# Stick attention with stationary values: fp32r value products over two query tiles, weights turned in two rounded parts

## The reference, cut to what matters

```python
for blk in range(S // SB_BLOCK):            # 8 blocks of 128 queries
    z = einsum('bthd,bshd->bhts', q[:, q0:kend], k[:, :kend]) * d ** -0.5
    strict = s_idx < t_idx
    log_beta = log_sigmoid(z)
    log_one_minus = where(strict, log_sigmoid(-z), 0.0)
    suffix = cumsum(log_one_minus, axis=3, reverse=True) - log_one_minus
    w = where(strict, exp(log_beta + suffix), 0.0)
    outs.append(einsum('bhts,bshd->bthd', w, v[:, :kend]))
```

## Time and profile before

| | |
|---|---|
| median of 2 runs | 2490.82 us (2488.91 to 2492.73) |
| profiled execution | 2491.72 us, its span 2489.9 us |
| mean granted TensorE clock over the span | 0.949 |
| busy over the span: PE, PEld | 2234.8 us (90%), 1854.2 us (74%) |
| busy over the span: DVE, ACT, POOL | 1336.9 us (54%), 1095.4 us (44%), 562.9 us (23%) |
| stick stage | first scores at 1620.67 us, last output copy at 1796.06 us |

### The profile page before, as it was taken

One profiled execution on the slowest core, in us unless ns is written; L12 is line 12 of the kernel. 1 busy time (PEld: TensorE's weight loads), 2 busy tenths in 40 slices (PEclk: granted clock), 3 DMA queues, 4 the chain that ended last, 5 costly groups with the idle time before them and its releaser, 6 DMA issues. The chain is left out here.

```text
span 2489.9 us, 34790 instructions
## 1 busy us (share of the span) xinstructions
PE 2234.8 (90%) x12528; PEld 1854.2 (74%) x12528; DVE 1336.9 (54%) x2212; ACT 1095.4 (44%) x2028; POOL 562.9 (23%) x598
## 2 busy tenths in 40 slices
PE   8997898899899899999589999688889999967778
PEld 6786787799887766676478887678777878856667
DVE  3332666688654666666541210777675434428843
ACT  3231545688632355554441210266543333328641
POOL 1002200723011122332210000466421000017821
PEclk9999899999999899999799999889989999988889
DMA  4686965633253599998553211453152543141152
GB/s 159 188 253 172 248 187 153 189 78 67 67 189 117 224 362 372 354 347 320 188 192 111 96 66 51 129 136 75 53 192 79 161 145 113 72 141 46 44 195 93
DMA packets 216904, 399.78 MB, mean 161 GB/s; under 512 B 90560, under 2 KB 111424, under 8 KB 204080
## 3 DMA queue, kind: packets, MB, share of 16 engines
q1 hardware_dynamic: 177184, 315.04, 39.9%
q10 hardware_dynamic: 28384, 61.62, 6.5%
q0 software_dynamic: 11184, 21.13, 2.4%
HBM read 300.68 MB, written 114.85 MB: 167 GB/s over the span
## 5 line engine op out<-in xcount | busy, mean ns | idle before, releaser
L78 PE MATMUL pe_acc<-pe_w,hT 128*128 128x512 f32 x960 | 229.5, 400 | 12.8 <-DVE hT L762 11.5
L78 PEld LDWEIGHTS pe_acc<-pe_w,hT 128*128 128x128 f32 x960 | 183.4, 192 | 55.9 <-DVE hT L762 14.1
L78 PE MATMUL ex_gu<-hT,ex_xT 128*128 128x512 f32 x792 | 196.4, 404 | 1.7 <-DVE hT L2666 1.7
L2666 DVE TENSOR_TENSOR hT<-ex_raw,hT 128x2048 fp32r<-128x2048 f32 x66 | 150.9, 2288 | 80.5 <-ACT hT L2637 80.5
L78 PE MATMUL pg_acc<-hT,pg_w 128*128 128x512 f32 x768 | 178.5, 393 | 0.9 <-DVE pg_w L286 0.9
L78 PEld LDWEIGHTS ex_gu<-hT,ex_xT 128*128 128x128 f32 x792 | 148.8, 191 | 35.9 <-DVE hT L2666 1.9
L78 PEld LDWEIGHTS pg_acc<-hT,pg_w 128*128 128x128 f32 x768 | 143.9, 188 | 34.1 <-issue 2.9
L2637 ACT ACTIVATE hT<-ex_raw 128x2048 fp32r<-128x2048 f32 x66 | 126.2, 1914 | 31.9 <-PEq L47 20.6
L325 DVE COPY pe_o<-pe_acc 128x512 f32<-128x512 f32 x28 | 19.3, 690 | 207.1 <-PE pe_acc L78 207.0
L2595 PE MATMUL ex_dn<-ex_wd,ex_hT 128*128 128x512 f32 x264 | 118.8, 593 | 0.8 <-ACT ex_hT L2631 0.8
L78 PE MATMUL pa_acc<-hT,pa_w 128*128 128x512 f32 (+1 forms) x432 | 100.6, 392 | 3.4 <-DVE pa_o L319 1.9
(11 more groups left out here) (545 smaller groups left out, 5355.2 us busy)
## 6 DMA issues: line engine op xcount, KB each, us to landing
ex_raw<-in_w_gate SPq DMA_DIRECT2D x33, 1024.0 KB, 7.3
ex_raw<-in_w_up SPq DMA_DIRECT2D x33, 1024.0 KB, 10.7
ex_wd<-in_w_down SPq DMA_DIRECT2D x33, 1024.0 KB, 13.7
ex_raw<-in_even_w_in SPq DMA_DIRECT2D x6, 2048.0 KB, 8.8
pg_raw<-in_odd_w_in SPq DMA_DIRECT2D x5, 2048.0 KB, 9.3
scr_q<-pa_o SPq DMA_DIRECT2D x32, 256.0 KB, 3.9
scr_k<-pa_o SPq DMA_DIRECT2D x32, 256.0 KB, 3.8
hT<-scr_k SPq DMA_DIRECT2D x16, 512.0 KB, 7.0
```

What stands on the lines that cost most here:

```text
L78: mm = pe.matmul(out, a(p, k), b(q, k), start=(k == 0 and i == 0), stop=(k == n - 1 and i == 2))
L2666: dve.tensor_tensor(split(s, LO)[:, :, g, :], raw[:, s % NW, g, :].rearrange("p (k n) -> p k n", k=8), split(s, HI)[:, :, g, :].bitcast(F3 ...
```

## The change

The value product is turned round. The values become the stationary operand: `vs` holds for each key block 128 columns, 64 of the values rounded to fp32r (ACT, 3149) and 64 of the remainder (POOL, 3239). The turned weights stream, as a rounded part that ACT writes (3170, 3173) and a remainder that DVE subtracts (3204, 3208). The product runs once for two query blocks, over 256 columns, in step T for the pair that ends with unit T-4, on odd steps (3123). On the last key block only the second query block streams, over 128 columns. The result has the two parts of the values in its partitions 0 to 63 and 64 to 127 and the queries in its columns. ACT drains it to `oT` (3163) one step later. TensorE turns it back and adds the two parts with a stacked identity (3134) in step T for the pair that ends with T-6. DVE copies both blocks to the output buffer in the step after (3224). The last step of a unit is thus three steps later than before.

```diff
--- before.py
+++ after.py
@@ -2988,7 +2988,10 @@
         be = st.sb("sb_be", [P, 4, S])
         pr = st.sb("sb_pr", [P, 2, S + 1])
         w = st.sb("sb_w", [P, 4, S])
-        wT = st.sb("sb_wT", [P, 2, S])
+        vs = st.sb("sb_vs", [P, 2, NT, 2 * DV], F32R)
+        wT = st.sb("sb_wT", [P, 2, 2, NT, 2 * P], F32R)
+        oT = st.sb("sb_oT", [P, 2, 2 * P])
+        stack = st.sb("sb_stack", [P, DV])
         ones = st.sb("sb_ones", [P, S])
         masks = st.sb("sb_masks", [P, 2, P])
         far = st.sb("sb_far", [P, P], F32R)
@@ -2996,20 +2999,30 @@
         o = st.sb("sb_ob", [P, 2, NT, DV])
         sps = [st.ps(f"sb_s{s}", [P, S]) for s in range(2)]
         tps = st.ps("sb_t", [P, S])
-        ops = [st.ps(f"sb_op{s}", [P, BANK]) for s in range(2)]
+        pvs = st.ps("sb_pv", [P, 2 * P])
+        ops = st.ps("sb_op", [P, 2, P])
...
+        def part_of(q, m, kk):
+
+            return wT[:, m // 2 % 2, q, kk, m % 2 * P:m % 2 * P + P]
+
+        def turned(kk):
+
+            return tps[:, kk.start * P:kk.stop * P].rearrange("p (k n) -> p k n", n=P)
 
         with nc.Block() as block:
             @block.sync
@@ -3046,7 +3059,7 @@
                         sp.sem_inc(passed, 1)
                         load_raw(h + 2, u)
                         store(h, u)
-                        sp.wait_ge(pv_done, h * T8 + T8)
+                        sp.wait_ge(vl_ok, h * T8 + T8)
                         sp.sem_inc(passed, 1)
                         load_v(h + 2, u)
                 store(heads - 2, 0)
@@ -3084,8 +3097,8 @@
                         m = (l - 3) % TURN
                         a, b = halves(m % T8)
                         reached(pe, w_ok, T - 2)
-                        reached(pe, wT_a, T - 3)
-                        reached(pe, wT_b, T - 3)
+                        reached(pe, wTl_a, T - 3)
+                        reached(pe, wTl_b, T - 3)
                         for k in range(b):
                             mm = pe.transpose(tps[:, k * P:(k + 1) * P], w[:, m % 4, k * P:(k + 1) * P], ident[:, :])
                             if k == a - 1 and b > a:
@@ -3096,19 +3109,31 @@
                             mm.then_inc(turned_a, 1)
                             pe.wait_ge(turned_a, T - 2)
                             pe.sem_inc(turned_b, 1)
-                    if active(T, 4, total):
-                        m = (l - 4) % TURN
-                        u, i = m // T8, m % T8
-                        if i == 0:
-                            pe.wait_ge(v_in[u], T - 4 - 8 * u + 16)
-                        reached(pe, o_done, T - 5)
-                        reached(pe, wT_a, T - 3)
-                        reached(pe, wT_b, T - 3)
+                    m = (l - 4) % TURN
+                    if active(T, 4, total) and m % 2 == 1:
+                        u, i, x = m // T8, m % T8, m // 2 % 2
+                        if i == 1:
+                            pe.wait_ge(vl_ok, T + 3)
+                        reached(pe, oT_ok, T - 5)
+                        reached(pe, wTl_a, T - 3)
+                        reached(pe, wTl_b, T - 3)
                         for k in range(i + 1):
-                            mm = pe.matmul(ops[m % 2][:, 0:DV], wT[:, m % 2, k * P:(k + 1) * P], v[:, u, k, :],
-                                           start=(k == 0), stop=(k == i))
-                        mm.then_inc(pv_done, 1)
-                tiles(pe, total, 8, 4, body)
+                            both = slice(P if k == i else 0, 2 * P)
+                            for q in (HI, LO):
+                                mm = pe.matmul(pvs[:, both], vs[:, u, k, :], wT[:, x, q, k, both], start=(k == 0 and q == HI),
+                                               stop=(k == i and q == LO), skip_group_check=True)
+                        mm.then_inc(pv_done, 2)
+                    m = (l - 6) % TURN
+                    if active(T, 6, total) and m % 2 == 1:
+                        x = m // 2 % 2
+                        if isinstance(T, int) and T == 7:
+                            pe.wait_ge(stack_ok, 3)
+                        reached(pe, oT_ok, T - 5)
+                        reached(pe, o_done, T - 7)
+                        for a in range(2):
+                            mm = pe.matmul(ops[:, a, 0:DV], oT[:, x, a * P:a * P + P], stack[:, :], start=True, stop=True)
+                        mm.then_inc(back, 2)
+                tiles(pe, total, 8, 6, body)
                 keep_clock(pe, sps[0], ident, 12)
 
             @block.scalar
@@ -3118,6 +3143,10 @@
                     act.wait_ge(raw_in[u], n_in)
                     act.activation(qs[:, u, :], qraw[:, u, :], ACT.Copy).then_inc(hi_ok, 4)
                     act.activation(kh[:, u, :], kraw[:, u, :], ACT.Copy).then_inc(hi_ok, 4)
+
+                def split_v(u):
+
+                    act.activation(vs[:, u, :, 0:DV], v[:, u, :, :], ACT.Copy).then_inc(vh_ok, T8)
 
                 def body(l, T):
                     if active(T, 0, total):
@@ -3127,21 +3156,36 @@
                         act.activation(be[:, l % 4, 0:n], sps[l % 2][:, 0:n], ACT.Sigmoid, scale=0.125).then_inc(be_ok, 1)
                         act.wait_ge(be_ok, T + 1)
                         act.activation(sps[l % 2][:, 0:n], sps[l % 2][:, 0:n], ACT.Sigmoid, scale=-0.125).then_inc(om_ok, 1)
+                    m = (l - 5) % TURN
+                    if active(T, 5, total) and m % 2 == 1:
+                        reached(act, pv_done, T - 4)
+                        reached(act, back, T - 8)
+                        act.activation(oT[:, m // 2 % 2, :], pvs[:, :], ACT.Copy).then_inc(oT_ok, 2)
                     if active(T, 3, total):
                         m = (l - 3) % TURN
                         a, b = halves(m % T8)
+                        if m % 2 == 0:
+                            reached(act, pv_done, T - 5)
+                        reached(act, turned_a, T - 2)
+                        act.activation(part_of(HI, m, slice(0, a)), turned(slice(0, a)), ACT.Copy).then_inc(wTh_a, 1)
                         reached(act, turned_b, T - 2)
                         if b > a:
-                            reached(act, pv_done, T - 4)
-                            act.activation(wT[:, m % 2, a * P:b * P], tps[:, a * P:b * P], ACT.Copy).then_inc(wT_b, 1)
+                            act.activation(part_of(HI, m, slice(a, b)), turned(slice(a, b)), ACT.Copy).then_inc(wTh_b, 1)
                         else:
-                            act.sem_inc(wT_b, 1)
+                            act.sem_inc(wTh_b, 1)
                     if active(T, 0, total):
                         if l % T8 == 3 and active(T + 5, 0, total):
 
                             u = 1 - l // T8
                             split_hi(u, (T + 5 - 8 * u) * 4 + 64)
-                tiles(act, total, 8, 4, body)
+                        if isinstance(T, int) and T < 2:
+                            act.wait_ge(v_in[T], 16)
+                            split_v(T)
+                        if l % T8 == 6 and active(T + 2, 0, total) and not (isinstance(T, int) and T < T8):
+                            u = 1 - l // T8
+                            act.wait_ge(v_in[u], T + 2 - 8 * u + 16)
+                            split_v(u)
+                tiles(act, total, 8, 5, body)
 
             @block.vector
             def _(dve):
@@ -3155,28 +3199,52 @@
                 def body(l, T):
                     if active(T, 3, total):
                         m = (l - 3) % TURN
-                        a, _ = halves(m % T8)
-                        reached(dve, turned_a, T - 2)
-                        reached(dve, pv_done, T - 4)
-                        dve.tensor_copy(wT[:, m % 2, 0:a * P], tps[:, 0:a * P]).then_inc(wT_a, 1)
+                        a, b = halves(m % T8)
+                        reached(dve, wTh_a, T - 2)
+                        dve.tensor_tensor(part_of(LO, m, slice(0, a)), turned(slice(0, a)), part_of(HI, m, slice(0, a)).bitcast(F32),
+                                          ALU.subtract).then_inc(wTl_a, 1)
+                        reached(dve, wTh_b, T - 2)
+                        if b > a:
+                            dve.tensor_tensor(part_of(LO, m, slice(a, b)), turned(slice(a, b)), part_of(HI, m, slice(a, b)).bitcast(F32),
+                                              ALU.subtract).then_inc(wTl_b, 1)
+                        else:
+                            dve.sem_inc(wTl_b, 1)
                     if active(T, 0, total):
                         n = widths[l % T8]
                         dve.wait_ge(om_ok, T + 1)
                         reached(dve, w_ok, T - 1)
                         dve.tensor_tensor_scan(pr[:, l % 2, S - n:S][:, ::-1], sps[l % 2][:, 0:n][:, ::-1], ones[:, 0:n], 1.0,
                                                ALU.mult, ALU.mult).then_inc(pr_ok, 1)
-                    if active(T, 4, total):
-                        m = (l - 4) % TURN
-                        u, i = m // T8, m % T8
```

(36 more changed lines are left out.)

## The result

| | before | after |
|---|---|---|
| median of 2 runs | 2490.82 us | 2598.10 us (2595.98 to 2600.21) |
| profiled execution, its span | 2491.72, 2489.9 us | 2595.98, 2593.9 us |
| mean granted TensorE clock | 0.949 | 0.935 |
| stick stage, first scores to last output copy | 175.6 us | 278.6 us |

A forecast was written before the change was run, and what follows sets the result against it. The loop scan, scores, sigmoids, scan was taken to end last, becoming one longer chain. Chain 33.1, first head 2.4, load 42.0, start 3.9, end 2.0, clock 15.9 + 2 on 2491.72 gave 2593.0, less 0.9: 2592 us, range 2562 to 2618.

The forecast's parts named there:

- load wait: Before the sigmoids of step 7, ACT waits for the DMA of the values: 7.0 us, six times, 42.0.
- steps 0, 1: Subtractions of tile 5, handover, seven turns, 12 products, turns back: 3.61 us a head, 2.65 more at half clock.
- steps 6, 7: Scores, sigmoids, drain, copies, rounded values, subtractions and scan in one chain: 9.94 us a head, besides the values' load.
- first head: Half the chain's cost, 2.4 us, as steps 0 to 2 lack earlier tiles, plus 3.9 for the second values.
- The chain: Side-by-side work becomes one chain round a head: 25.8 against 21.1 us, 4.7 a head, 33.1 over seven heads.
- rival 1: TensorE's relief decides, with copies and loads hidden: 2486 us, not slower; chance 0.03.
- The clock: After each values' wait, half clock in steps 0 and 1 adds 2.65 us, six times 15.9; short waits add 2.
- 2 for the short waits: The clock allowance for short waits, beside the 15.9 after the values' waits: 2 us in all.
- rival 4: The clock stays low well beyond step 1: 2605 to 2626 us; chance 0.16.
- The start: In step 1 ACT waits for the second values, ahead of the sigmoids of step 2: 3.9 us.
- The end: After the last scan, the last tiles pass through turn, copy, subtraction, products, drain, turns back and copy: 2.0 us more.
- The signs: Blocks 0 of heads 3 to 8 about 33 to 36 us apart, head 8 about 26; six ACT waits near 7 us.

The follow-up runs named there:

- e1: The changed kernel with the values of head h+2 loaded ahead of the store of head h on SP; 2551.07 us, ratio 1.0249.
- e7: e1 without DVE's subtractions, still 40 products a head, the high parts multiplied twice; 2517.62 us, ratio 1.0095.
- e6: e1 with subtractions kept but low parts of the turned weights not multiplied, 20 products a head, not 40; 2545.75 us, ratio 1.0213.
- e2: The changed kernel with 24 throwaway TensorE matmuls in the load waits of heads 3 to 8, and also in head 2; 2602.80 us, ratio 1.0440.
- e9: The changed kernel with 24 throwaway TensorE matmuls only in the load waits of heads 3, 5 and 7; 2596.56 us, ratio 1.0432.
- e3: e1 with DVE's scan of each step made ahead of that step's two subtractions; 2571.84 us, ratio 1.0331.

## Why the prediction was right

The four legs of a head, from the starts and ends of the rows above. "Full clock" are the shortest values of e1 in heads 3 to 7, where no load wait stands in them; they come from different heads, and no head of e1 had all four (its shortest took 27.59 us). Before, steps 2, 3 and 4, 5 are 5.83 and 4.03 us, the other four steps 11.2.

| leg | forecast | full clock (e1) | after, head 5 |
|---|---|---|---|
| steps 0, 1 (last scan's end to scores of step 2) | 3.61 + 2.65 clock | 3.89 | 5.51 |
| steps 2, 3 | 6.75 | 6.88 | 6.88 |
| steps 4, 5 | 5.54 | 5.64 | 5.64 |
| steps 6, 7 | 9.94 + 7.0 load | 9.88 | 17.34 |
| head | 25.8 + 9.65 | 26.3 | 35.4 |

| term | forecast | measured |
|---|---|---|
| chain, seven heads | 33.1 | 36.6 = 7 x 26.29 - 147.4 |
| values' load, six times | 42.0 | 43.4 = 42.8 of idle + 6 x 0.09 |
| clock | 15.9 + 2 | 16.6, what is left of 244.0 - 147.4 |
| start of the stage | 0 | 2.3 |
| first head | 3.9 + 2.4 | 2.2 |
| end | 2.0 | 4.2 = (1901.58 - 1889.85) - 7.5 |
| behind the stage | 0 | -1.3 |
| sum | 101.3 | 104.0 |

- **The chain** was right to 0.5 us a head, and each leg to 0.3. e7 confirms its largest part, the subtractions. The rule in the Trainium skill ("Perfetto Trace Analysis", "Identifying the Most-Contended Engine") to relieve the fullest engine first would have given rival 1's 2486. Here the fullest engine was relieved, at the price of work for the others, and the time rose by 107 us; e6 shows what TensorE's work is worth on this chain, 5 to 8 us for half of the products.
- **The load wait** was right in place, number and size. e1 removes it.
- **The clock** was right in sum by luck and wrong in cause, which is the step of the prediction that failed: the turns, products and turns back of steps 0 and 1 "come next on the chain; at half clock they add 2.65, six times 15.9". They did not double: in e1 the turns took 1.6 times as long, the products 1.8 times, and the turns back, by which time the clock was rising again, no longer (1706 to 1708 stood at 0.50, 1709.5 to 1710 at 1.00). From scan to the scores of step 2 the changed kernel took 4.86 to 5.60 us in heads 3 to 8, 7.9 above six times 3.89, half of the 15.9. But the clock falls in every head at least once, in short idle times of the new chain, with or without the load wait: in e1 the remainder that I put down to it is 11 us over heads 2 to 8 (their 195.1 us against 7 x 26.29). So "2 for the short waits" was far too little, and the two errors cancelled. The load wait's own share would be the rest, some 5 or 6; no run isolates it, and e2, less its 4 us in head 2, got nothing back. The Trainium skill's warning of short idle times between groups of matmuls ("TensorE: Matmul & The Clock Gate", "A second HAM failure mode: psum-queue depth-cycling"), which I had given to rival 4, is what e9's windows agree with.
- **The start** was over-estimated. The wait for the second values was 2.32 us, not 3.9, and head 1 grew by 2.2 instead of 6.3: it is slow before, too, with its clock at 0.50 from 1626 to 1634. That the stage began 2.3 us later says nothing: in the profiled executions of e3 and e2, with the same program ahead of the stage, it began at 1616.8 and 1630.7.
- **The end** had its turn (1.73) and product (2.21) at a granted clock of 0.55 to 0.59; I had counted them at full. By the rows of e1 that is some 1.3 of the 2.2 us missed; the rest was not taken apart.
- **The signs** that I named: blocks 0 of heads 3 to 8 stand 35.2 to 38.2 us apart (33 to 36 forecast), and by their last scans heads 3 to 7 are 35.1 to 38.1. The largest is head 3, outside the forecast: its clock fell a second time and was 0.50 from 1694 to 1704. Head 8 is 27.9 (26).

## To carry to other kernels

An engine that leads in busy time is not therefore the one to relieve: ask whose result the next instruction waits for, and whether the relief adds a hand to that chain. A second pass over a single buffer by another engine (copy, then subtract) makes a loop of three engines that no order tried here removed. When a consumer moves to an earlier step, follow its transfer through the whole in-order queue, past every store that it now stands behind.

## What I had not expected of the hardware

Giving TensorE work in a long idle time kept its clock at 1.00 there and gained nothing, since it fell in the next short ones: busy 0.61 and 0.74 of 2 us, then a clock of 0.61 over the next 2 us. Taking work off TensorE lowered its clock (0.90 to 0.80 over 160 us from e1 to e6), and steps 6 and 7 took up to 11.0 us instead of 9.88: 40 products a head with fewer waits (e7) were 28 us faster than 20 with them (e6).
